# First norms applied where their products are read out of PSUM, and a new loading order

## What is computed

```python
def rmsnorm(x, g):
    xf = x.astype(jnp.float32)
    y = xf * lax.rsqrt(jnp.mean(xf * xf, axis=-1, keepdims=True) + NORM_EPS)
    return (y * g.astype(jnp.float32)).astype(x.dtype)

mkv = rmsnorm(mem, mem_norm_g) @ w_mem_kv          # product 0, 512 columns
hn = rmsnorm(h, pre_mix_g[0])                      # h is x at first
proj = hn @ nsa_w_in[0]                            # products 1 to 5, 512 columns each, the last 164
```

## Time and profile before

| what | value |
|---|---|
| median of 3 runs | 829.43 us (829.42 to 832.85) |
| profiled execution, its own time | 832.04 us |
| its span, first to last instruction | 830.3 us |
| TensorE busy | 751.4 us, 90% |
| VectorE busy | 489.3 us, 59% |
| ScalarE busy | 407.0 us, 49% |
| mean granted TensorE clock | 0.956 |
| data from HBM | 109.68 MB, 133 GB/s over the span |

### The profile page before, as it was taken

The page is one execution under the profiler, slowest core; times in us unless marked ns, Lnnn a source line. Parts: engine busy times, 40 slices in busy tenths (PEclk is TensorE's granted clock), DMA queues, the critical chain, the costliest instruction groups (busy, mean ns, idle before and its releaser), DMA issues.

```text
span 830.3 us, 15555 instructions
## 1 busy us (share of the span) xinstructions
PE 751.4 (90%) x6725; PEld 652.4 (79%) x6725; DVE 489.3 (59%) x705; ACT 407.0 (49%) x642; POOL 98.1 (12%) x148
## 2 busy tenths in 40 slices
PE   4999878679999999999888887999869999999997
PEld 3888755468888888888878775999758888888885
DVE  5677656633876666544759795333535766666432
ACT  6644745524855554533874713433214855455511
POOL 4003044520000000000511003800000000000000
PEclk9999879889999999999979988999969999999999
DMA  9846610003655655554723521000015465555521
GB/s 302 290 120 212 207 52 2 1 1 115 215 186 172 201 182 175 200 203 137 241 91 103 178 85 44 5 4 4 4 35 194 157 198 189 171 199 189 182 85 52
DMA packets 78279, 111.74 MB, mean 135 GB/s; under 512 B 2124, under 2 KB 63714, under 8 KB 78210
## 3 DMA queue, kind: packets, MB, share of 16 engines
q1 hardware_dynamic: 77090, 107.67, 39.2%
q0 software_dynamic: 976, 3.04, 1.2%
q10 hardware_dynamic: 144, 0.04, 0.0%
HBM read 109.68 MB, written 1.05 MB: 133 GB/s over the span
## 4 chain that ended last, share of the span: by engine, by line
PE 65%; DVE 15%; ACT 8%; issue 2%; POOL 0%; DVEq 0%; ACTq 0%
PE ps L942 18%; PE ps L1081 10%; PE ps L944 9%; PE ps L665 8%; PE ps L667 7%; PE ps L666 7%; DVE w_lo L1667 3%; ACT scores L1306 2%; ACT w_hi L1240 2%; PE ps L820 1%; DVE row_max L1747 1%; PE ps L794 1%; DVE x_hi_lo L1884 1%; ACT x_hi_lo L1411 1%; PE ps L862 0%
## 5 line engine op out<-in xcount | busy, mean ns | idle before, releaser
L1667 DVE TENSOR_TENSOR w_lo<-w_raw,w_hi 128x2048 fp32r<-128x2048 f32 (+1 forms) x101 | 227.4, 2264 | 109.4 <-ACT w_hi L1240 109.3
L942 PE MATMUL ps<-x_hi_lo,w_hi 128*128 128x512 f32 x640 | 226.5, 399 | 0.0
L1240 ACT ACTIVATE w_hi<-w_raw 128x2048 fp32r<-128x2048 f32 (+1 forms) x101 | 189.3, 1891 | 60.3 <-PE ps L667 57.3
L944 PE MATMUL ps<-x_hi_lo,w_lo 128*128 128x256 f32 x640 | 179.7, 281 | 0.0
L942 PEld LDWEIGHTS ps<-x_hi_lo,w_hi 128*128 128x128 f32 x640 | 120.3, 188 | 29.8
L944 PEld LDWEIGHTS ps<-x_hi_lo,w_lo 128*128 128x128 f32 x640 | 120.9, 189 | 0.0
L665 PE MATMUL ps<-w_hi,x_hi_lo 128*128 128x512 f32 (+2 forms) x240 | 84.2, 351 | 5.9 <-DVE x_hi_lo L1884 3.0
L666 PE MATMUL ps<-w_lo,x_hi_lo 128*128 128x512 f32 (+2 forms) x240 | 82.6, 344 | 0.0
L667 PE MATMUL ps<-w_hi,x_hi_lo 128*128 128x512 f32 (+2 forms) x240 | 82.6, 344 | 0.0
L665 PE MATMUL ps<-w_hi,hidden_hi 128*128 128x512 f32 x176 | 68.6, 390 | 0.0
L666 PE MATMUL ps<-w_lo,hidden_hi 128*128 128x512 f32 x176 | 68.5, 389 | 0.0
(11 more groups left out here) (366 smaller groups left out, 1147.8 us busy)
## 6 DMA issues: line engine op xcount, KB each, us to landing
w_raw<-w_ffn_in SPq DMA_DIRECT2D x44, 1024.0 KB, 5.1
w_raw<-w_ffn_out SPq DMA_DIRECT2D x22, 1024.0 KB, 5.0
w_raw<-rwkv_w_in SPq DMA_DIRECT2D x11, 1024.0 KB, 5.4
w_raw<-nsa_w_in SPq DMA_DIRECT2D x8, 1024.0 KB, 11.6
w_raw<-w_out SPq DMA_DIRECT2D x8, 1024.0 KB, 5.1
w_raw<-w_mem_kv SPq DMA_DIRECT2D x2, 1024.0 KB, 8.7
w_raw<-nsa_cmp_k_w SPq DMA_DIRECT2D x2, 1024.0 KB, 5.6
w_raw<-nsa_cmp_v_w SPq DMA_DIRECT2D x2, 1024.0 KB, 5.6
```

The source lines that it names most:

```text
L942: pe.matmul(psum[:, bank + j, :], kt_of(w_hi, i, k)[:, c], xx[:, k, :, :].rearrange("p c n -> p (c n)"), start=k == 0, stop=False)
L944: ins = pe.matmul(psum[:, bank + j, 0:SEQ], kt_of(w_lo, i, k)[:, c], xh[:, k, :], start=False, stop=k == KD - 1)
L1240: act.activation(w_hi[:, i % SPL, 0:size(i)], raw[:, i % RAW, 0:size(i)], ACT.Copy).then_inc(hi_done, 1)
L1667: dve.tensor_tensor(w_lo[:, i % RAW, 0:size(i)], raw[:, i % RAW, 0:size(i)], w_hi[:, i % SPL, 0:size(i)], ALU.subtract).then_inc(lo_done, 1)
```

## The change

The rows are turned as they were loaded, without norm. The squares, roots and inverses are taken later, into buffers of their own (`first_rms`, `first_rinv`), and the inverse of a row is applied when the product is read from PSUM, in `token_out`, for product 0 with the memory's and for products 1 to 5 with the input's. The input's turns move to between the halves of product 0. The squares' by-product goes to an SBUF buffer and no longer to PSUM. ScalarE takes a first Sqrt of a constant early, splits piece 0 before it waits for `vec_ev`, and does the squares of the input behind piece 2. SP's order becomes piece 0, memory, piece 1, `rows_b`, input.

```diff
--- before.py
+++ after.py
@@ -237,8 +237,11 @@
         cmx = at(oo, "block_max", [P, HEADS]); oo += 64
         csum = at(oo, "block_sum", [P, HEADS]); oo += 64
         ccf = at(oo, "block_coef", [P, HEADS]); oo += 64
+        rms0 = at(oo, "first_rms", [P, 2, TT]); oo += 32
+        rin0 = at(oo, "first_rinv", [P, 2, TT]); oo += 32
         ident_r = at(oo, "ident_rounded", [P, P], F32R); oo += 512
         cmask_r = at(oo, "causal_mask_rounded", [P, 2, P], F32R); oo += 1024
+        junk = at(PH + 4 * TT * NSA_IN, "squares", [P, TT, D])
         rt = at(o_hn + 6656, "rope_tmp", [P, 4 * 48])
         rtq = at(PH + 4 * TT * NSA_IN + 12288, "rope_tmp_q", [P, 4, TT, HEADS, HALF])
 
@@ -313,7 +316,7 @@
         s_dve = sem("dve_chain")
         s_act = sem("act_chain")
         n_sqA, n_sqD, n_rms, n_inv = sem("n_sqA"), sem("n_sqD"), sem("n_rms"), sem("n_inv")
-        n_scA, n_scD, n_tp, n_hi, n_lo = sem("n_scA"), sem("n_scD"), sem("n_tp"), sem("n_hi"), sem("n_lo")
+        n_tp, n_hi, n_lo = sem("n_tp"), sem("n_hi"), sem("n_lo")
         vec_tp, vec_ev = sem("vec_tp"), sem("vec_ev")
         tok_mm, tok_evA, tok_evD = sem("tok_mm"), sem("tok_evA"), sem("tok_evD")
         trig_r, trig_s = sem("trig_arg"), sem("trig_done")
@@ -427,11 +430,11 @@
                     sp.wait_ge(used, i - RAW + 1)
                 sp.dma_start(raw_view(i), pieces[i]).then_inc(landed[i % RAW], 16)
 
+            load_piece(0)
             sp.dma_start(hn[:], mem[0].rearrange("(t p) d -> p t d", p=P)).then_inc(in_mem, 16)
+            load_piece(1)
             for item in LOADS_B:
                 rows(sp, *item)
-            load_piece(0)
-            load_piece(1)
             sp.dma_start(h[:], x[0].rearrange("(t p) d -> p t d", p=P)).then_inc(in_x, 16)
             for i in range(2, NPIECES):
                 load_piece(i)
@@ -666,16 +669,18 @@
                 pe.matmul(dst, ah, bl, start=False, stop=False)
                 return pe.matmul(dst, al, bh, start=False, stop=stop)
 
-            def norm(n):
-                for t in range(TT):
-                    pe.wait_ge((n_scA, n_scD)[t], n + 1)
-                    for b in range(KD // 2):
-                        for j in range(2):
-                            k = 2 * b + j
+            def input_turns(n):
+                pe.wait_ge((in_mem, in_x)[n], 16)
+                if n:
+                    pe.wait_ge(n_lo, 4)
+                src = (hn, h)[n]
+                for b in range(KD // 2):
+                    for j in range(2):
+                        k = 2 * b + j
+                        for t in range(TT):
                             ins = pe.transpose(psum[:, b, j * SEQ + t * P:j * SEQ + (t + 1) * P],
-                                               hn[:, t, k * P:(k + 1) * P], ident[:])
-                        if t:
-                            ins.then_inc(n_tp, 1)
+                                               src[:, t, k * P:(k + 1) * P], ident[:])
+                    ins.then_inc(n_tp, 1)
 
             def norm_tile(m, t):
                 for half in range(2):
@@ -711,6 +716,8 @@
                 i0 = first["mem"] if g == 0 else first["nsa"] + 2 * (g - 1)
                 n = pieces[i0].shape[2]
                 for hf in range(2):
+                    if hf and g == 0:
+                        input_turns(1)
                     if hf and between is not None:
                         between()
                     pe.wait_ge(lo_done, i0 + hf + 1)
@@ -726,8 +733,6 @@
                                         start=kk == 0, stop=kk == KD - 1)
                         if hf == 1 and t == 0:
                             ins.then_inc(tok_mm, 1)
-                            if g == 0:
-                                norm(1)
                     ins.then_inc(used, 1)
 
             def turn(k):
@@ -972,7 +977,7 @@
             pe.wait_ge(in_vec, 16 * N_VEC)
             pe.transpose(psum[:, 7, 0:NA], rowsA[:], ident[0:NA, 0:NA])
             pe.transpose(psum[:, 7, P:P + NB], rowsB[:], ident[0:NB, 0:NB]).then_inc(vec_tp, 1)
-            norm(0)
+            input_turns(0)
             token_gemm(0, mh, ml)
             for g in range(1, 4):
                 token_gemm(g, xh, xl)
@@ -1240,31 +1245,15 @@
                     act.activation(w_hi[:, i % SPL, 0:size(i)], raw[:, i % RAW, 0:size(i)], ACT.Copy).then_inc(hi_done, 1)
                 split[0] = max(split[0], min(n, NPIECES))
 
-            def norm(n):
-                src = hn if n == 0 else h
-                if n == 0:
-                    act.wait_ge(in_mem, 16)
-                elif n == 1:
-                    act.wait_ge(in_x, 16)
-                    act.wait_ge(n_lo, 4)
-                    act.wait_ge(n_tp, 4)
-
-                act.activation(psum[:, 0:2, :], src[:, 0, :].rearrange("p (b n) -> p b n", b=2), ACT.Square,
-                               accum_out=ssq[:, 0:1]).then_inc(n_sqA, 1)
-                if n == 0:
-                    act.wait_ge(consts, 2)
+            def squares(n):
+                act.wait_ge((in_mem, in_x)[n], 16)
+                act.activation(junk[:, 0, :], (hn, h)[n][:, 0, :], ACT.Square, accum_out=ssq[:, 2 * n:2 * n + 1]).then_inc(n_sqA, 1)
+
+            def roots(n):
                 for t in range(TT):
                     act.wait_ge((n_sqA, n_sqD)[t], n + 1)
-                    act.activation(rms[:, t:t + 1], ssq[:, t:t + 1], ACT.Sqrt, bias=cst[:, 0:1], scale=1.0 / D).then_inc(n_rms, 1)
-                    if t == 0:
-                        act.wait_ge(n_inv, TT * n + 1)
-                        act.activation(hn[:, 0, :], src[:, 0, :], ACT.Copy, scale=rin[:, 0:1]).then_inc(n_scA, 1)
-                if n == 0:
-                    split_to(1)
-                    act.wait_ge(vec_ev, 1)
-                elif n == 1:
-                    split_to(3)
-                norm_hi(n)
+                    act.activation(rms0[:, n, t:t + 1], ssq[:, 2 * n + t:2 * n + t + 1], ACT.Sqrt, bias=cst[:, 0:1],
+                                   scale=1.0 / D).then_inc(n_rms, 1)
 
             def norm_hi(n):
                 dh = mh if n == 0 else xh
@@ -1278,8 +1267,10 @@
 
             def token_out(g):
                 act.wait_ge(tok_mm, g + 1)
+                n = min(g, 1)
+                act.wait_ge(n_inv, TT * n + 1)
                 dst = mkv[:, 0, :] if g == 0 else pr[:, 0, 512 * (g - 1):min(512 * g, NSA_IN)]
-                act.activation(dst, psum[:, 4 + 2 * (g % 2), 0:dst.shape[1]], ACT.Copy).then_inc(tok_evA, 1)
+                act.activation(dst, psum[:, 4 + 2 * (g % 2), 0:dst.shape[1]], ACT.Copy, scale=rin0[:, n, 0:1]).then_inc(tok_evA, 1)
 
             def turn_out(k):
 
@@ -1460,10 +1451,18 @@
 
             for item in LOADS_A:
                 rows(act, *item)
-            norm(0)
+            act.wait_ge(consts, 2)
+            act.activation(cst[:, 7:8], cst[:, 0:1], ACT.Sqrt)
+            split_to(1)
+            act.wait_ge(vec_ev, 1)
+            norm_hi(0)
             split_to(2)
-            norm(1)
+            squares(0)
+            roots(0)
+            norm_hi(1)
             split_to(3)
+            squares(1)
+            roots(1)
             token_out(0)
             split_to(4)
             act.wait_ge(trig_r, 1)
@@ -1668,26 +1667,15 @@
                                       ALU.subtract).then_inc(lo_done, 1)
                 split[0] = max(split[0], min(n, NPIECES))
 
-            def norm_start(n):
-                src = hn if n == 0 else h
-                if n == 0:
-                    dve.wait_ge(in_mem, 16)
-                elif n == 1:
-                    dve.wait_ge(in_x, 16)
-                    dve.wait_ge(n_tp, 4)
-                if n:
-                    dve.wait_ge(n_lo, 4 * n)
-                dve.tensor_tensor_reduce(psum[:, 2:4, :].rearrange("p b n -> p (b n)"), src[:, 1, :], src[:, 1, :], 1.0, 0.0,
-                                         ALU.mult, ALU.add, ssq[:, 1:2]).then_inc(n_sqD, 1)
-
-            def norm(n):
-                src = hn if n == 0 else h
-                norm_start(n)
+            def squares(n):
+                dve.wait_ge((in_mem, in_x)[n], 16)
+                dve.tensor_tensor_reduce(junk[:, 1, :], (hn, h)[n][:, 1, :], (hn, h)[n][:, 1, :], 1.0, 0.0,
+                                         ALU.mult, ALU.add, ssq[:, 2 * n + 1:2 * n + 2]).then_inc(n_sqD, 1)
+
+            def inverses(n):
                 for t in range(TT):
                     dve.wait_ge(n_rms, TT * n + t + 1)
-                    dve.reciprocal(rin[:, t:t + 1], rms[:, t:t + 1]).then_inc(n_inv, 1)
-                dve.wait_ge(n_inv, TT * (n + 1))
-                dve.tensor_scalar(hn[:, 1, :], src[:, 1, :], rin[:, 1:2], None, ALU.mult).then_inc(n_scD, 1)
+                    dve.reciprocal(rin0[:, n, t:t + 1], rms0[:, n, t:t + 1]).then_inc(n_inv, 1)
 
             def norm_lo(n):
                 dl, dh = (ml, mh) if n == 0 else (xl, xh)
@@ -1703,8 +1691,10 @@
             def token_out(g):
```

(11 more changed lines are left out.)

## The result

The changed kernel takes 835.49 us (median of 5 runs, 834.63 to 837.59), the kernel before 829.63 us in the same comparison (5 runs, 829.42 to 832.85). The ratio is 1.0048, with a 95% interval of 1.0025 to 1.0071. The forecast was 834.2 with a range of 829.2 to 838.0, a loss of 4.8 us; by the two ratios the loss is 4.0 and 3.1 us. The medians alone lie 5.9 and 2.8 us apart: five runs of a kernel whose own runs spread over 3 us and more don't fix the size, so the loss stands at 1.8 to 5.9 us, the outer ends of the two intervals. The profiled execution of the changed kernel took 834.63 us where 836.8 was forecast for it, its span 832.9 where 835.1 was forecast.

What follows compares the result with a forecast made beforehand. TensorE bounds the kernel, so its opening stage counts: 3.5 later start, 1.7 back from the clock, waits 1.0 + 0.9 + 1.5 less 0.46, +4.7, taken as 4.8. 829.43 + 4.8 = 834.2 us, range 829.2 to 838.0.

Steps and rivals of the forecast that it cites:

- What the start waits for: Opening stage: TensorE's first turn waits for all row loads, now behind 3 MB; from 8.8 to 15.0 us.
- V: Time of TensorE's first turn, of the rows of constants: 8.8 us before, 15.0 forecast, bounds 11.2 and 16.4.
- Rival 1: Row loads land early, V stays near 9, no change in total time, 829.4 us; chance 0.16.
- The page on queues: SP's queue: completion isn't first-in first-out, so rows could land before piece 1's last share, perhaps 1 us off the sum.
- From V to the first product: Turns on TensorE take 4.3 us, VectorE's work 4.2; first product at 19.4 against 15.92, 3.5 us later.
- The clock: TensorE's first matmuls: without a pause ahead, clock high from the first product on, or nearly; 1.7 us back.
- The splits: TensorE waits for split weights ahead of pieces 2, 3 and 4: 1.0, 0.9 and 1.5 us, against 0.46 before.
- The whole shift stays: Behind piece 4: same work in the same order, so the opening stage's 4.8 us remains to the end.
- rival 3: Behind 80 us: a low-clock stretch disappears while rows land early, giving about 826 us; chance 0.06.
- The free edits: Squares to SBUF, scaled output on VectorE, early Sqrt: hidden, cost nothing; under 0.3 us together if uncovered.

Runs made afterwards that it cites:

- e1: Changed kernel with SP's eight row loads moved ahead of the memory, behind piece 0 only; ratio 0.9997 to the kernel before.
- e10: e6 with the changed kernel's loading order, row loads behind 3 MB; ratio 0.9999 to the kernel before.
- e9: e6 with SP's eight row loads issued by ScalarE behind its own five; ratio 0.9969 to the kernel before.
- e7: Changed kernel unchanged, measured again with more runs; 835.46 us, ratio 1.0037 to the kernel before.
- e8: Kernel before, unchanged, run again for a second profile; ratio 0.9994 to the kernel before.
- e2: Changed kernel with SP's old loading order: memory, row loads, pieces 0 and 1, input; ratio 1.0034 to the kernel before.
- e4: Changed kernel with squares, roots and inverses of the input moved behind the splits of pieces 3 to 7; ratio 1.0011 to the kernel before.
- e3: Kernel before with only SP's loading order changed to piece 0, memory, piece 1, row loads, input; ratio 1.0022 to the kernel before.
- e6: e5 with piece 2 split ahead of the input's high and low parts, pieces 4 and 5 ahead of position arithmetic and sine; ratio 0.9930 to the kernel before.
- e11: e6 unchanged, measured again with more runs; ratio 0.9929 to the kernel before.
- e5: Changed kernel with the edits of e1 and e4 together; ratio 0.9962 to the kernel before.

## Why the prediction was right

- *What the start waits for.* V = 15.0 was forecast because the row loads have in front of them what the queue had "up to piece 1 before: 3 MB and eight row loads"; 15.13 measured, piece 1 at 14.8. e1 and e10 move nothing but these loads and shift the first turn by 6.1 and 5.6 us. The bounds 11.2 and 16.4 were wider than needed; that the middle came within 0.13 us is partly luck. Rival 1 (rows land early) is out. (A slip in the range: by the prediction's own steps its lower end, V = 13.4 with the full gain of the clock, is +3.2 us and not +2.8. Nothing hangs on it.)
- *The page on queues.* By the Trainium skill, "DMA: Bandwidth & Descriptors", section "Queues, rings and completion order", I allowed that the rows pass piece 1. They landed after it. The same section of the Trainium skill says that each DMA engine goes round between queues packet by packet. The trace of e9 agrees in so far as packets of ScalarE's queue ran beside those of SP's, but the last came only at 12.4 us: it did not bring the rows in early here, 13.23 on a queue of their own.
- *From V to the first product.* Forecast V + 4.3 from the turns and V + 4.2 from VectorE; measured 4.42, with 0.16 of it a wait for the low parts of the memory. As forecast, both ended together.
- *The clock.* Forecast: high from the first product on, "or nearly", 1.7 us back. Measured: from 19.55 to 25.41 24 matmuls took 5.86, so 0.4 was lost and 1.3 came back (7.17 before); in the second pair, e7 and e8, 0.7 came back (6.18 and 6.87). The step is right, its size 0.4 to 1.0 too large. The reason given, no pause between turns and products, fits all 14 profiles as told at e2, though none moves the pause and nothing else.
- *The splits.* The starts of pieces 2, 3 and 4 were forecast at 33.2, 39.6 and 46.6; 33.26, 39.44 and 46.43 came. The waits themselves were forecast as 1.0, 0.9 and 1.5 and stand in the rows as 0.47, 0.44 and 1.22. Part of that is only how idle time is counted, from the modelled end of the last matmul, which lies some 0.16 behind the time when the next could have started. The rest column gives their worth without that: 2.30 us more than before, where the forecast added 2.94. Of the 0.6 between them 0.4 is that TensorE came later to the turns of x than forecast (25.41 for 25.0), so it had less to wait, and 0.2 that the low parts of pieces 3 and 4 were ready 0.2 earlier. e4 takes the second and third wait away and gets 2.15 us in the rest.
- *The whole shift stays.* This is the step that held least. In e7 against e8 it stays to 500 us, within 0.2; behind that the clock's low stretches differ, as rival 3 had it for single stretches, and 2.7 us were given back. In the first pair of profiles the shift had risen to 6.2 by 200 us, the pitch of the feed-forward stage took off 2.0, and low stretches behind 500 us another 1.9, to 2.3 at the end. So both pairs kept about half of the 4.6 to 4.8 us of the opening stage, where "the whole shift stays" was forecast; the two intervals put the loss at 1.8 to 5.9 us, which allows the whole shift as well as half of it. Likewise e3, e4, e6, e9 and e10 came out 1 to 2 us better than their piece 4 says, e11 3.6. Whether a shifted start meets those low stretches at a better place, or this is spread between executions, I could not settle; no experiment here held the later clock fixed.
- *The free edits.* The scaled output on VectorE takes 0.75 where the copy took 0.68, ScalarE's squares 1.06 to 1.11 with 1.03 before; both covered.

The chances stood at 0.46 for slower by over 0.5% and 0.48 for within 0.5%; a forecast of 4.8 us is 0.58%, just over that bound, and the measured 0.48% and 0.37% lie just under it. On which side a single comparison falls was left open by the prediction, and is luck.

## What to carry to other kernels

Before an operation is taken off the path to the first product, ask which of its inputs comes last without it. Here removing a norm brings the first product 1.3 to 1.5 us forward (e1, e5; 2.9 was forecast had the rows stayed early), but small loads that every engine waits for were moved behind megabytes and cost more. When a queue's order is changed, list for each load who waits for it, and put the small ones that gate everything ahead of the large ones that gate one step (e1, e10). Once the start is early, what is split for the next matmuls goes ahead of work whose result is read much later: that was worth 2.2 us here (e5) and 2.9 (e6, e11), counted in the rest, against 21.02 in e1. And split such a stage into parts that repeat between profiles and parts that don't before a difference is given to an edit (e4).

## What the runs showed of the hardware

- Small loads did not pass large ones by using another engine's queue: 8 loads of 3 to 10 KB issued by ScalarE between 3.7 and 6.8 us let TensorE start at 13.23; the same loads issued by SP between 1.3 and 4.1 us, behind 1 MB, at 9.15 (e9, e6). With the same times of issue, ScalarE's own five loads had their last packet at 8.8 us beside 3 MB of SP's queue (changed kernel) and at 5.7 in e6.
- A pause behind an early burst on TensorE goes with slower products behind it: the granted clock was 0.50 over 16 to 22 us in e2, behind a pause of 3.5 us, and the first 24 matmuls took 8.44 us, against 5.86 in the changed kernel without a pause. Over 14 profiles: 6.87 to 8.44 us with a pause of 2.2 to 3.5 us, 5.55 to 6.75 with at most 1.42.
- The paired matmuls of the first feed-forward stage run at a pitch of 0.347 or of 0.353 us, by the execution: 2.0 us of the whole, half of the effect studied here.
